# Weight blocks through a ring of four: ScalarE rounds the high half, VectorE writes the low half over the raw block

## The reference, cut to what matters

```python
for layer in (0, 1):
    hn = rms_norm(h, mix_norm[layer])
    h = h + (lru_dilated_mixer(hn, ...) if layer == 0 else swa_sink_mixer(hn, ...))
    hn = rms_norm(h, xa_norm[layer])
    h = h + memory_cross_attention(hn, rms_norm(mem, xa_mem_norm[layer]), xa_wq, xa_wkv, xa_wo)
    h = h + swiglu(rms_norm(h, ffn_norm[layer]), ffn_w_gate_up, ffn_w_down)
return rms_norm(h, final_norm)
```

## Time and profile before

| | |
|---|---|
| median of 3 launches | 1483.05 us (1481.87 to 1483.18) |
| profiled execution: its own time, first to last instruction | 1481.1 us |
| TensorE busy | 1394.9 us, 94% |
| VectorE busy | 753.8 us, 51% |
| ScalarE busy | 343.8 us, 23% |
| GpSimd busy | 872.5 us, 59% |
| mean granted TensorE clock | 0.969 |

### The profile page before, as it was taken

One profiled execution on the slowest core, in us unless ns is written; L12 is line 12 of the kernel. 1 busy time (PEld: TensorE's weight loads), 2 busy tenths in 40 slices (PEclk: granted clock), 3 DMA queues, 4 the chain that ended last, 5 costly groups with the idle time before them and its releaser, 6 DMA issues.

```text
span 1481.1 us, 17229 instructions
## 1 busy us (share of the span) xinstructions
PE 1394.9 (94%) x6296; PEld 1131.8 (76%) x6296; DVE 753.8 (51%) x875; ACT 343.8 (23%) x718; POOL 872.5 (59%) x576
## 2 busy tenths in 40 slices
PE   5999956999999999999999988999999999999997
PEld 4888745578777888888888777877777888888886
DVE  5876999504748344004333888827564442023332
ACT  4326204511233111001111214632331110001122
POOL 4666645446555666666666655346565666666662
PEclk9999987999999999999999997999999999999998
DMA  5232321013222332233323321013222332333221
GB/s 194 81 114 85 100 64 57 16 57 124 85 73 75 100 96 91 97 100 100 99 93 93 105 94 44 1 43 100 71 71 86 93 94 97 100 100 98 91 96 57
DMA packets 90239, 127.14 MB, mean 86 GB/s; under 512 B 5440, under 2 KB 53824, under 8 KB 90176
## 3 DMA queue, kind: packets, MB, share of 16 engines
q1 hardware_dynamic: 90176, 126.27, 26.9%
HBM read 124.15 MB, written 2.10 MB: 85 GB/s over the span
## 4 chain that ended last, share of the span: by engine, by line
PE 78%; DVE 17%; issue 3%; ACT 1%; DMA 0%; SPq 0%; DVEq 0%; ACTq 0%
PE ps L494 22%; PE ps L497 22%; PE ps L498 22%; PE ps L622 4%; PE ps L589 4%; DVE acc L845 3%; PE ps L605 2%; DVE rope L892 2%; DVE rope L891 1%; DVE h L863 1%; DVE z_lo L839 1%; DVE xc L1097 1%; DVE lru_d L1087 1%; DVE xc L1095 1%; DVE rope L890 1%
## 5 line engine op out<-in xcount | busy, mean ns | idle before, releaser
L443 POOL TENSOR_TENSOR w_lo<-raw,w_hi 128x1024 fp32r<-128x1024 f32 x222 | 555.9, 2504 | 18.5
L441 POOL TENSOR_SCALAR w_hi<-raw 128x1024 fp32r<-128x1024 f32 x222 | 250.4, 1128 | 489.9 <-issue 350.5
L494 PE MATMUL ps<-z_hi,w_hi 128*128 128x512 f32 x1072 | 426.5, 398 | 6.2 <-DVEq L885 3.0
L497 PE MATMUL ps<-z_lo,w_hi 128*128 128x512 f32 x1072 | 421.3, 393 | 0.0
L498 PE MATMUL ps<-z_hi,w_lo 128*128 128x512 f32 x1072 | 421.1, 393 | 0.0
L494 PEld LDWEIGHTS ps<-z_hi,w_hi 128*128 128x128 f32 x1072 | 204.2, 190 | 52.3 <-issue 5.0
L497 PEld LDWEIGHTS ps<-z_lo,w_hi 128*128 128x128 f32 x1072 | 204.3, 191 | 44.9 <-issue 2.7
L494 PE MATMUL ps<-f_hi,w_hi 128*128 128x512 f32 x608 | 238.2, 392 | 0.2 <-DVEq L1004 0.2
L498 PE MATMUL ps<-f_hi,w_lo 128*128 128x512 f32 x608 | 236.7, 389 | 0.0
L498 PEld LDWEIGHTS ps<-z_hi,w_lo 128*128 128x128 f32 x1072 | 203.7, 190 | 43.1
L497 PE MATMUL ps<-f_lo,w_hi 128*128 128x512 f32 x608 | 236.6, 389 | 0.0
(11 more groups left out here) (162 smaller groups left out, 1263.1 us busy)
## 6 DMA issues: line engine op xcount, KB each, us to landing
raw<-in_w_gate_up SPq DMA_DIRECT2D x176, 256.0 KB
raw<-in_w_down SPq DMA_DIRECT2D x44, 512.0 KB
raw<-in_w_in SPq DMA_DIRECT2D x28, 512.0 KB
raw<-in_w_out SPq DMA_DIRECT2D x20, 512.0 KB
raw<-in_xa_wkv SPq DMA_DIRECT2D x16, 512.0 KB
raw<-in_xa_wq SPq DMA_DIRECT2D x8, 512.0 KB
raw<-in_xa_wo SPq DMA_DIRECT2D x8, 512.0 KB
raw<-in_w_qkv SPq DMA_DIRECT2D x8, 512.0 KB
```

The lines of the kernel that those rows point to most:

```text
L441: pool.tensor_scalar(w_hi[:, half], raw[:, j], 1.0, 1.0, ALU.mult, ALU.mult).then_inc(s_hi, 1)
L443: pool.tensor_tensor(w_lo[:, half], raw[:, j], w_hi[:, half].bitcast(F32), ALU.subtract).then_inc(s_split, 1)
L494: ins = pe.matmul(o, whi, rhi, start=start, stop=False)
L497: pe.matmul(o, whi, rlo, start=False, stop=False)
```

## The change

There are now four slots. Slot u % 4 holds the raw block of unit u and its rounded half `w_hi`; the low half is written over the raw block (`w_lo` is the same memory as `raw`). ScalarE rounds (`high_part`: one ACTIVATE Copy of 128 x 1024), VectorE subtracts (`low_part`: one TENSOR_TENSOR of 128 x 1024, after ScalarE), TensorE waits for `s_lo`. The load of unit u waits until TensorE has begun unit u - 3. GpSimd keeps only `normalise`. Where in their order ScalarE and VectorE do this is written out by hand: `high_to(u)` and `low_to(u)` do all units below u that haven't been done, and calls of them stand between the existing operations. The load of mask m0 moves up in SyncE's order, ahead of the last of attn0's four units.

```diff
...
+FIRST_TURN = {0: 1, 1: 2, 3: 3, 5: 4, 7: 6}
+
+
+def split_turns(second, end):
+
+    return {-1: second + 3, 0: min(second + 4, end + 2), 1: min(second + 5, end + 2), 2: min(second + 6, end + 2),
+            3: end + 2, 5: end + 3, 7: end + 4, DB: end + 6}
...
-        w_hi = at("w_hi", [P, SPLIT, 2, 512], F32R, z_wh)
-        w_lo = at("w_lo", [P, SPLIT, 2, 512], F32R, z_wl)
+        w_hi = at("w_hi", [P, SLOTS, 2, 512], F32R, z_wh)
+        w_lo = at("w_lo", [P, SLOTS, 2, 512], F32R, z_raw)
...
-                if u_static >= RAW:
-                    sp.wait_ge(s_split, u - RAW + 1)
+                if u_static >= SLOTS:
+                    sp.wait_ge(s_used, u - SLOTS + 2)
...
-            def split(u, j, empty=False):
-
-                half = j % SPLIT
-                pool.wait_ge(s_raw[j], (u - j + RAW) * (32 // RAW))
-                if not empty:
-                    pool.wait_ge(s_used, u - SPLIT + 2)
...
+            def low_part(u, u_static):
+
+                slot = u_static % SLOTS
+                dve.wait_ge(s_hi, u + 1)
+                dve.tensor_tensor(w_lo[:, slot], raw[:, slot], w_hi[:, slot].bitcast(F32), ALU.subtract).then_inc(s_lo, 1)
...
+                if done:
+                    low_to(turn[-1])
 
                 for m in range(DB if done else 0):
                     dve.wait_ge(done, m + 1)
...
                         if m >= lag:
                             low(m - lag)
+                    low_to(turn.get(m, 0))
                 if norm_next:
                     for m in range(DB - lag if done else 0, DB):
                         low(m)
...
+                if done:
+                    low_to(turn[DB])
...
                 for n in range(H + 4):
                     if n < H:
                         maxima(n)
+                    if n == 0:
+                        low_to(u0 + 4)
...
                     if n == 1:
-                        for i in range(a["dve_splits"]):
-                            split(UNIT0[a["name"]] + 2 + i)
+                        low_to(u0 + 5)
                         if n in extra:
                             extra[n]()
+                        low_to(u0 + 6)
                         for b in range(2):
                             dve.wait_ge(a["s_filler"], b + 1)
...
+                    if n == 2:
+                        low_to(u0 + 7)
                     if 2 <= n < H + 2 and a["turned_first"]:
                         turned(n - 2)
...
+                    if n == 5:
+                        low_to(u0 + 8)
...
             for m in range(DB):
                 decay(m)
+                if m % 2:
+                    low_to(UNIT0["in_qkv"] + 4 + m // 2 + 1)
...
             for t in range(4):
                 qk_tile(t)
+                low_to(UNIT0["in_qkv"] + 8 + t + 1)
...
             for t in range(4, 8):
                 qk_tile(t)
+                low_to(UNIT0["attn0"] + t - 4 + 1 if t < 7 else 0)
...
                     for t in range(4):
                         qkv1(q1[:, t, :], s_done["qkv_q0"], "qkv_q0", t, t)
+                        low_to(q1_unit + 2 + t // 2 + 1)
                     for t in range(4):
                         rotate_q(t)
+                        low_to(q1_unit + 4 + t // 2 + 1)
+                    low_to(q1_unit + 7)
...
                     memory_low(1)
+                    low_to(q1_unit + 9)
                     rotate_q(4)
...
                     rotate_q(5)
+                    low_to(UNIT0["attn1"] + 4)
...
+                        low_next(0)
                         for p in range(2):
                             dve.wait_ge(s_ff, 4 * n + p + 3)
                             dve.tensor_tensor(ff_u[:, p, :], ps[:, b0 + 2 + p, :], rstd[:], ALU.mult).then_inc(s_ff_up, 1)
...
+                        low_next(1)
                         for p in range(2):
                             dve.wait_ge(s_ff_silu, 2 * n + p + 1)
...
+                        low_next(2)
+                        low_next(3)
...
+            def high_part(u, u_static):
+
+                slot = u_static % SLOTS
+                act.wait_ge(s_raw[slot], 32 * (u_static // SLOTS + 1) + (u - u_static) * (32 // SLOTS))
+                act.activation(w_hi[:, slot], raw[:, slot], ACT.Copy).then_inc(s_hi, 1)
...
+                high_to(turn.get(-1, 0))
                 for m in range(DB):
...
+                    high_to(turn.get(m, 0))
+                high_to(turn.get(DB, 0))
                 act.wait_ge(s_sum, NORM[norm] + 1)
...
                     if n == H - 1 and not a["masks"]:
                         act.nop().then_inc(s_free[GROUP0[a["name"]] % 2], 4)
+                    high_to(u0 + {0: 4, 1: 5, 2: 7, 5: 8}.get(n, 0))
                     if extra and n in extra:
                         extra[n]()
+                    if n == 1:
+                        high_to(u0 + 6)
```

More of the change, by code:

```diff
@@ L51 @@
 BANK = 512
-RAW = 4
-SPLIT = 2
+SLOTS = 4
 CHUNK = (12, 10)
@@ L408, in _ @@
                     sp.dma_start(m1[:], mask1).then_inc(s_mask1, 16)
-                stream(f"attn{l}", xa_wkv[l], 4, count=1)
                 if l == 0:
-                    sp.wait_ge(s_done["in_qkv"], 12)
-                    sp.dma_start(m0[:], mask0).then_inc(s_mask0, 16)
+                    for j in range(4):
+                        if j == 3:
+                            sp.wait_ge(s_done["in_qkv"], 12)
+                            sp.dma_start(m0[:], mask0).then_inc(s_mask0, 16)
+                        unit(UNIT0["attn0"] + j, [(0, 512, rows(xa_wkv[0], 2 * P * j, 0))])
+                else:
+                    stream("attn1", xa_wkv[1], 4, count=1)
                 stream(f"out{l}", (w_out0, w_out1)[l], (6, 4)[l])
@@ L832, in _, with low_to, residual @@
             link = chain.link
-            def residual(norm, done, bias=None, group0=0, norm_next=True):
+            told = [0]
+            def low_part(u, u_static):
+                slot = u_static % SLOTS
+                dve.wait_ge(s_hi, u + 1)
+                dve.tensor_tensor(w_lo[:, slot], raw[:, slot], w_hi[:, slot].bitcast(F32), ALU.subtract).then_inc(s_lo, 1)
+            def low_to(u1):
+                for u in range(told[0], min(u1, UNITS)):
+                    low_part(u, u)
+                told[0] = max(told[0], min(u1, UNITS))
+            def residual(norm, done, bias=None, group0=0, norm_next=True, units=()):
+                turn = split_turns(*units) if done else {}
                 def low(m):
@@ L873, in residual @@
                         low(m)
+                        if not done:
+                            low_to(FIRST_TURN.get(m, 0))
+                if done:
+                    low_to(turn[DB])
             def one_over_rms(norm):
@@ L1082, in _ @@
                 dve.tensor_tensor(xc[:, m, :], gate_i[:, m % 2, :], xc[:, m, :], ALU.mult).then_inc(s_gx, 1)
+                if m % 2:
+                    low_to(UNIT0["in_qkv"] + m // 2 + 1)
             def decay(m):
@@ L1132, in _ @@
             attention(ATTN["attn0"], {0: lambda: late_recurrence(4), 1: lambda: late_recurrence(6)})
-            residual("xa0", s_done["out0"], group0=GROUP0["out0"])
+            residual("xa0", s_done["out0"], group0=GROUP0["out0"], units=(UNIT0["out0"] + 6, UNIT0["xq0"]))
             for l in (0, 1):
@@ L1173, in _ @@
                     attention(ATTN["attn1"], {1: lambda: [rotate_q(6), rotate_q(7)]})
-                    residual("xa1", s_done["out1"], bias="b_out", group0=GROUP0["out1"])
+                    residual("xa1", s_done["out1"], bias="b_out", group0=GROUP0["out1"],
+                             units=(UNIT0["out1"] + 4, UNIT0["xq1"]))
                 one_over_rms(f"xa{l}")
@@ L1234, in _, with high_to, residual @@
         def _(act):
-            def residual(norm):
+            told = [0]
+            def high_part(u, u_static):
+                slot = u_static % SLOTS
+                act.wait_ge(s_raw[slot], 32 * (u_static // SLOTS + 1) + (u - u_static) * (32 // SLOTS))
+                act.activation(w_hi[:, slot], raw[:, slot], ACT.Copy).then_inc(s_hi, 1)
+            def high_to(u1):
+                for u in range(told[0], min(u1, UNITS)):
+                    high_part(u, u)
+                told[0] = max(told[0], min(u1, UNITS))
+            def residual(norm, units=None):
+                turn = split_turns(*units) if units else FIRST_TURN
                 def high(dst, m):
@@ L1301, in attention @@
                 H = a["heads"]
+                u0 = UNIT0[a["name"]]
                 def exps(n):
@@ L1396, in _ @@
                 rec_high(m)
+            high_to(UNIT0["attn0"] + 3)
             def extra0(m, dst, src):
@@ L1409, in _ @@
             attention(ATTN["attn0"], {0: lambda: extra0(4, mem2_hi, mem_hi), 1: lambda: extra0(6, mem2_lo, mem_lo)})
-            residual("xa0")
+            residual("xa0", (UNIT0["out0"] + 6, UNIT0["xq0"]))
             for l in (0, 1):
```

115 lines of the change are left out of this document (58 added, 57 removed).

## The result

The changed kernel takes 1498.55 us (median; 1495.3 to 1500.26) where the kernel before took 1482.46 on the same chip (1481.76 to 1483.18): ratio 1.011, 95% interval 1.0097 to 1.0124. The profiled execution took 1497.28 us, its span 1495.5.

What follows compares the result with a forecast made beforehand. TensorE (busy 94%) was taken as the bound. Terms 4.0 - 3.9 + 13.2 + 2.0 + 7.3 + 1.0 - 5.0 gave +18.6, taken as +18 on 1483.05: 1501 us, range 1480 to 1515 us.

Steps and rivals of the forecast that it cites:

- up to attn0's scores of head 3: Through attn0's early heads: VectorE's waits for rounding outweigh an earlier maxima(0), so these scores start 4.0 us later.
- n = 5 of both: At n = 5 of attn0 and attn1: one more VectorE wait, half hidden by a head's slack, +1 us together.
- norm sums of xa0 and xa1: Norm sums after out0 and out1: TensorE's waits and the slow clock behind them go, -3.9 and -5.0 us.
- both cross-attentions: At n = 2, VectorE waits for rounding ahead of the copy that TensorE's values need; +13.2 us for two.
- norm sums of ffn0, ffn1: Norm sums after xo0 and xo1: the group has only two units, so +1.0 us each, +2.0 together.
- mix1 to values(0) of attn1: attn1 and its prelude: norm sum wait gone (-2.5), later VectorE waits; values of head 0 come 7.3 us later.
- start and tail: Kernel's start and tail: subtractions behind squared tiles, but contention gone; 0 us, bounds -2 and +3.
- the 4.4 us step: Cross-attentions at n = 2: VectorE stands 4.4 us for exponentials, rounding and subtraction ahead of the copy for values.
- A: Attentions: ScalarE rounds early enough to hide VectorE's waits, contention decides; -15 us, 1468 us; chance 0.17.
- B: Attentions: half of the losses (26 becomes 11) against unchanged gains; within 3 us of before; chance 0.06.
- C: Feed-forward stages: TensorE starved, each of 22 groups losing 1 us; +22 more, 1523 us; chance 0.07.
- D: Four attentions: subtraction and GpSimd's normalise lock each other out, 1.2 us each, up to +14, 1515 us; chance 0.08.

Runs made afterwards that it cites:

- e2: Changed kernel with VectorE's subtraction of the block due at n = 2 moved behind its copy of the turned probabilities; 1482.67 us, 1.0008 of the kernel before.
- e1: Changed kernel with ScalarE rounding the attention blocks due at n = 0, 1, 2, 5 ahead of its exponentials; 1468.25 us, 0.9908 of the kernel before.
- e3: Changed kernel with each attention's eighth block (due at n = 5) rounded and subtracted at n = H + 1; 1489.82 us, 1.0054 of the kernel before.
- e7: As e1 on the changed kernel, but the eighth block (n = 5) is rounded behind the exponentials; 1476.49 us, 0.9976 of the kernel before.
- e6: Changed kernel plus GpSimd arithmetic for every block on a pad of its own; 1554.68 us, 1.0497 of the kernel before.
- e5: Kernel before with four slots, low half over the raw block and loads gated by TensorE's use; GpSimd still splits; 1474.52 us, 0.9952 of the kernel before.

## Why the prediction was right, point by point

The number (1501 for 1498.55) is nearer than its terms were, and that is luck: errors of about 10 us one way and 14 the other offset each other. By the table, and the tail after its last row (+16.9 there, +14.4 at the end of the span):

| Term | predicted | measured |
|---|---|---|
| up to attn0's scores of head 3 | +4.0 | -0.2 |
| n = 5 of both | +1 | +3.4 and +7.0 |
| norm sums of xa0 and xa1 | -3.9, -5.0 | -4.0, -6.5 |
| both cross-attentions | +13.2 | +6.9 and +6.8 |
| norm sums of ffn0, ffn1 | +2.0 | +0.7, 0.0 |
| mix1 to values(0) of attn1 | +7.3 | +2.8 |
| start and tail | 0 | start inside the first row, tail -2.5 |

**Cross-attentions**: right in place, mechanism and size. The lines above show the 4.4 us step; e2 and e1 take most of it away. Of the 6.9 us in xattn0, 4.4 are gone when the first values start (5.1 foreseen) and the rest goes in slower matmuls behind the wait (1.5 foreseen).

**Mis-sized: n = 5.** "Half hidden by the slack of a head: +1" was 10.4. The slack was there and hid part (VectorE waits 2.36 us and subtracts 1.23 in attn1, TensorE waits 2.11), but two terms were too small: what is left of the wait, some 2 in each, and the half clock behind it, which I had charged after the long waits at n = 2 and not here. e3 takes 8.7 us off the changed kernel, and e7, which puts this block behind the exponentials again, is 10 us slower than e1.

**Mis-sized the other way: what VectorE gets back.** I gave the start 0 and it gave -2.6 by the first norm sum, although TensorE's first weight product waits 4.6 us where it waited 2.4: no 2.8 us step is left in the first norm. In e6, with GpSimd busy, -0.5 of it stays. `maxima(0)` came 7.5 us earlier (222.54 for 230.07), not 5.0, since the start's share was left out. From there to the scores of head 3 attn0 then lost 7.3 for my 9.0 (the prediction has 8.9, but 27.8 + 15.5 - 6.5 is 36.8). Mix1's norm sum gave 5.0 for 2.5. In e6 the gain of xa1's norm sum and what follows, up to xattn1's first scores, is 2.5 for 6.5. The prediction put the gain at the norm sums down to freed contention. How much of it is that stays open: e5 gains 2.3, 2.9 and 4.6 of the 4.0, 5.0 and 6.5 us with GpSimd splitting and an accumulation of 1582 ns. The errors offset each other: 9.4 too little loss at n = 5 and 0.5 in the cross-attentions; 4.2, 4.5, 1.5, 1.3 and 2.5 too little gain elsewhere.

**Removed and added.** The subtraction took 1225 ns for 1.22 foreseen, never more than 1229; the rounding 1057 for 1.05. In the feed-forward stages nothing moved.

**Rivals.** A (contention decides) asked ScalarE to be early; it isn't by the order given, and e1, which makes it so, lands where A said 1468: 1468.25. So A's condition was false in the changed kernel. That e1 fits its number bears A out only in part: e1 still loses 1.3 to 2.3 us in each attention where A had no loss, and how much of the gain is contention stays open. B (half of the attention losses) didn't occur: the rows of the table for the attentions add up to 26.7 us where 25.5 were predicted. B's own sum was off as well: half of 26 would leave 13 and not 11. C didn't occur. D: in the changed kernel no subtraction runs at the same time as a normalisation, so it was never put to the test there; the subtractions never stretched, and the longest normalisation is 0.70 us. In e1 six normalisations that start while a subtraction runs take 0.9 to 1.4 us longer than their like; where the subtraction is the later of the two, it takes up to 1.55 us for 1.22. The longest takes 1.77 us, where one of 128 x 128 has a mean of 0.37 in the changed kernel. It runs beside the subtraction shown under it and the operation of the recurrence behind that:

```profile
240.26 1.77 POOL L445 TENSOR_SCALAR prob<-prob,stat 128x128 f32<-128x128 f32 x1 [239.81 <-DVE stat L947]
```

```profile
240.08 1.20 DVE L808 TENSOR_TENSOR w_lo<-raw,w_hi 128x1024 fp32r<-128x1024 f32 x1
```

So the lock exists and weighs about 1 us a time; the Trainium skill (SBUF — State Buffer, "Who interferes with whom") says the two exclude each other, and e1's row agrees. The prediction gave that rule too simply: in that section the Trainium skill frees a VectorE instruction with one SBUF input only outside the modes that use both ports. The copy of `sq` into `acc` has one input, and with GpSimd quiet it became shorter all the same. Its row, first before, then changed:

```profile
L843 DVE COPY acc<-sq 128x512 f32<-128x512 f32 x7 | 8.5, 1218 | 0.2 <-ACT sq L1257 0.2
```

```profile
L827 DVE COPY acc<-sq 128x512 f32<-128x512 f32 x7 | 2.9, 421 | 0.2 <-DVE h L848 0.2
```

## What to carry to other kernels

Work that nobody wants soon still costs its full wait when it stands ahead of something wanted now, on an engine that works in order. When work moves to a busier engine, place each piece twice: where its input is ready (the producer ahead of its own long work), and behind whatever the bottleneck is waiting for. Here the same instructions cost +1.1% in one order and gave -1.5% in another.

## What the runs showed of the hardware that I had not expected

25 us around the same 2.1 us wait in attn1 had a mean granted clock of 0.73, 0.93 or 1.00. What decides between them isn't settled: the three kernels differ in what TensorE did before (its wait ahead of the values of head 0 was 12.4 us in the changed kernel, 7.7 in e7, 8.3 in e2). GpSimd work on a pad that nobody reads made the whole program 4% slower than without it (1498.55 to 1554.68); VectorE's operations with two SBUF inputs became longer (the accumulation 685 to 962 ns), and how much the late normalisations add wasn't separated.
